# Splitting the weights of 96 projection slabs into high and low parts

## The reference

```python
def first_block(x, ...):
    h = rms_norm(x, norm_gain)
    proj = h @ w_in                                 # 2048 x 8192
    h_conv, b_gate, c_gate, z_conv, q, k, v, z_attn = split(proj)   # 8 parts of 1024
    y_conv = short_gated_conv(h_conv, b_gate, c_gate, conv_w)       # 3 taps
    y_conv = rms_norm(y_conv, conv_out_gain) * silu(z_conv)
    y_attn = attention(rms_norm(q), rms_norm(k), v)                 # 8 heads, causal, 256 keys
    y_attn = rms_norm(y_attn, attn_out_gain) * silu(z_attn)
    return x + concat([y_conv, y_attn]) @ w_out     # 2048 x 2048

def second_block(x, ...):
    h = rmsnorm(x, norm_mix)
    proj = h @ w_in_2                               # 2048 x 7168: conv, state space, gates
    branch_conv = conformer_conv(proj[...])         # 31 taps, layer norm, @ conv_w_out
    branch_ssm = s5_ssm(proj[...])                  # scan, then @ w_val and @ w_gate
    x = x + (gates_a * branch_conv + gates_b * branch_ssm) @ w_out_2
    h = rmsnorm(x, norm_ffn)
    return rmsnorm(x + peer(h), norm_final)         # @ w_q, keys, 128 experts' rows a token from u and v
```

## Time and profile before

| | |
|---|---|
| time, median of 3 runs | 2801.74 us (2801.71 to 2801.96) |
| the profiled execution, its own time | 2801.38 us |
| its span, first to last instruction | 2799.3 us |
| mean granted TensorE clock | 0.869 |
| PE busy | 1950.2 us, 70% |
| DVE busy | 1589.6 us, 57% |
| ACT busy | 279.8 us, 10% |
| POOL busy | 892.0 us, 32% |

### The profile page before, as it was taken

One profiled execution on the slowest core, in us unless ns is written; L12 is line 12 of the kernel. 1 busy time (PEld: TensorE's weight loads), 2 busy tenths in 40 slices (PEclk: granted clock), 3 DMA queues, 4 the chain that ended last, 5 costly groups with the idle time before them and its releaser, 6 DMA issues. The chain is left out here.

```text
span 2799.3 us, 21816 instructions
## 1 busy us (share of the span) xinstructions
PE 1950.2 (70%) x7892; PEld 1459.8 (52%) x7892; DVE 1589.6 (57%) x2475; ACT 279.8 (10%) x593; POOL 892.0 (32%) x525
## 2 busy tenths in 40 slices
PE   8999999999999999999994000077775000057776
PEld 6888888888887888888783000032222000022222
DVE  5012223110886896520157999977547999964444
ACT  1002222101102010200110000000001000000000
POOL 0000000000000000000004888856555888865553
PEclk9999999999998999999997555599998555589999
DMA  7554554554453554455456999999999999999998
GB/s 184 151 149 123 141 143 135 137 149 121 120 151 90 154 146 152 136 163 153 120 134 247 422 422 422 422 421 422 422 422 386 423 422 422 422 421 422 421 421 341
DMA packets 458269, 747.06 MB, mean 267 GB/s; under 512 B 22130, under 2 KB 391236, under 8 KB 392260
## 3 DMA queue, kind: packets, MB, share of 16 engines
q0 software_dynamic: 73728, 536.90, 46.1%
q1 hardware_dynamic: 373248, 207.63, 26.4%
q10 hardware_dynamic: 11204, 1.29, 0.3%
HBM read 743.68 MB, written 2.10 MB: 266 GB/s over the span
## 5 line engine op out<-in xcount | busy, mean ns | idle before, releaser
L366 PE MATMUL ps<-operand,weight_raw 128*128 128x256 f32 x6144 | 1348.9, 382 | 10.0 <-DVE operand L885 9.0
L366 PEld LDWEIGHTS ps<-operand,weight_raw 128*128 128x128 f32 x6144 | 1173.5, 192 | 177.4 <-issue 15.7
L594 PE MATMUL ps<-weight_raw,residual_t 128*128 128x512 f32 x256 | 124.0, 630 | 676.0 <-ACT residual_t L839 637.1
L1316 DVE SCALAR_TENSOR_TENSOR slots<-slots,work 128x2048 f32<-128x2048 f32 x192 | 437.5, 2291 | 29.4 <-DMA slots<-in_peer_u,slots 29.0
L594 PEld LDWEIGHTS ps<-weight_raw,residual_t 128*128 128x128 f32 x256 | 48.5, 199 | 751.4 <-ACT residual_t L839 697.7
L594 PE MATMUL ps<-slots,residual_t 128*128 128x512 f32 x768 | 356.3, 608 | 116.5 <-DMA slots<-in_peer_v,slots 116.0
L326 POOL DMA_INDIRECT slots<-in_peer_u,slots x192 | 395.8, 2062 | 60.5 <-issue 58.9
L319 POOL IOTA slots<- 128x16 f32 x1 | 0.1, 144 | 1232.9 <-DVE operand L1236 1232.9
L1331 DVE SCALAR_TENSOR_TENSOR work<-slots,work 128x2048 f32<-128x2048 f32 x96 | 225.7, 2351 | 220.5 <-DMA slots<-in_peer_v,slots 220.2
L326 POOL DMA_INDIRECT slots<-in_peer_v,slots x192 | 262.4, 1366 | 180.8 <-PE ps L594 143.5
L594 PEld LDWEIGHTS ps<-slots,residual_t 128*128 128x128 f32 x768 | 140.4, 192 | 331.9 <-ACT residual_t L839 170.4
(11 more groups left out here) (197 smaller groups left out, 1078.0 us busy)
## 6 DMA issues: line engine op xcount, KB each, us to landing
weight_raw<-in_w_in SPq DMA_DIRECT2D x120, 1024.0 KB, 6.1
weight_raw<-in_w_out SPq DMA_DIRECT2D x32, 1024.0 KB, 6.0
weight_raw<-in_peer_w_q SPq DMA_DIRECT2D x16, 1024.0 KB, 6.0
weight_raw<-in_ssm_w_val SPq DMA_DIRECT2D x8, 1024.0 KB, 5.2
weight_raw<-in_ssm_w_gate SPq DMA_DIRECT2D x8, 1024.0 KB, 5.2
weight_raw<-in_conv_w_out SPq DMA_DIRECT2D x8, 1024.0 KB, 5.2
slots<-in_peer_u,slots POOLq DMA_INDIRECT x192, 16.5
slots<-in_peer_v,slots POOLq DMA_INDIRECT x192, 15.9
```

The lines of the kernel that those rows point to most:

```text
L366: mm = nc.tensor.matmul(ps_p[:, t % PSLOTS, :], w[:, k, :], operand[:, k, :], start=(k == order[0]), stop=(k == order[-1]))
L594: mm = nc.tensor.matmul(ps_v[:, c, :], diag[:, n, :], rows[n][:, c * 512:(c + 1) * 512], start=False, stop=False, skip_group_check=True)
L1316: v.scalar_tensor_tensor(out=rows[n], in0=rows[n], scalar=1.0, in1=h_tok[:, t, :], op0=ALU.mult, op1=ALU.mult, accum_out=dots[:, at:at + 1 ...
```

## The change

96 of the 192 slabs are computed in another way: the 64 of the first input projection and the 16 of each output projection. A weight w is split into a high part (w stored as float32r, a float32 type of lower precision for products) and a low part (w minus the high part), and so is the operand; the product is then high x high + high x low + low x high. The low x low part is left out.

- ScalarE copies each slab from `weight_raw` to one of two new buffers `weight_high` (`split_high`), always two tiles ahead, and GpSimd writes the low part over the slab itself (`weight_low` lies at the address of `weight_raw`).
- The operand's high part goes to `operand_high`, at the address of `op_b`, by 16 copies on ScalarE; the low part to `operand_low`, in place in `op_a`, by 16 subtractions: on GpSimd for the first stage, on VectorE for the two output projections. For the first output projection the products y stay in their slots instead of going to `op_b`.
- TensorE (`split_product`) issues per tile 32 products of the high weights and then, when the low slab is there, 16 of the low weights.
- The order of the input projection's parts is changed (the gate c before the gate b), the gated convolution of three taps is cut up and its first two parts stand after heads 6 and 7, and TensorE turns the state-space coefficients after tile 14 instead of after tile 23.
- `operand` and the slabs lie next to each other in SBUF, with `weight_high` behind them; the other 96 slabs keep float32.

```diff
+NHIGH = 2
+SPLIT_IN, SPLIT_OUT, SPLIT_OUT2 = 0, 64, 80
+SLAB_OUT2 = 64 + 16 + 56 + 16 + 8
+def split_slab(i):
+    return i if i < SPLIT_OUT2 else SLAB_OUT2 + i - SPLIT_OUT2
-Q0, K0, V0, ZA0, HC0, BG0, CG0, ZC0 = range(0, 64, 8)
+Q0, K0, V0, ZA0, HC0, CG0, BG0, ZC0 = range(0, 64, 8)
+LAM_AFTER = 14
+        with nc.sbuf_tensor("weight_low", [P, NSLAB, SLAB], F32R) as w_low, \
+                nc.sbuf_tensor("operand_low", [P, KD, T], F32R) as o_low, \
+                nc.sbuf_tensor("operand_high", [P, KD, T], F32R) as o_high:
+            pass
         w_raw = sb("weight_raw", [P, NSLAB, SLAB])
+        opnd = sb("operand", [P, 2, KD, T])
+        w_high = sb("weight_high", [P, NHIGH, SLAB], F32R)
...
# GpSimd: ahead of the mask, then behind it
+            for k in range(KD):
+                pool.wait_ge(o_high_ready, k + 1)
+                nc.gpsimd.tensor_tensor(o_low[:, k, :], op_a[:, k, :], o_high[:, k, :], ALU.subtract).then_inc(o_low_ready, 1)
...
+            for i in range(SPLIT_OUT2 + KD):
+                s = split_slab(i)
+                pool.wait_ge(w_high_ready, i + 1)
+                nc.gpsimd.tensor_tensor(w_low[:, s % NSLAB, :], w_raw[:, s % NSLAB, :], w_high[:, i % NHIGH, :],
+                                        ALU.subtract).then_inc(w_low_ready, 1)
...
# TensorE
+            def split_product(i, order=None, ready=None):
+                t = split_tile(i)
...
+                pe.wait_ge(w_high_ready, i + 1)
+                pe.wait_ge(proj_freed, t + 1)
+                for k in order:
+                    if ready is not None:
+                        pe.wait_ge(o_low_ready, ready(k))
+                    nc.tensor.matmul(out, high[:, k, :], o_high[:, k, :], start=(k == order[0]), stop=False)
+                    nc.tensor.matmul(out, high[:, k, :], o_low[:, k, :], start=False, stop=False)
+                pe.wait_ge(w_low_ready, i + 1)
+                for k in order:
+                    mm = nc.tensor.matmul(out, low[:, k, :], o_high[:, k, :], start=False, stop=(k == order[-1]))
+                mm.then_inc(proj_done, 1)
...
             for t in range(24):
-                tile(TILE_IN, t, op_a, ready=(lambda k: (h_scaled, k + 1)) if t == 0 else None)
+                split_product(SPLIT_IN + t, ready=(lambda k: k + 1) if t == 0 else None)
+                if t == LAM_AFTER:
+                    pe.wait_ge(ssm_coef, 1)
...
# ScalarE
+            def split_high(i):
+                s = split_slab(i)
+                act.wait_ge(raw_landed[s % NSLAB], 16 * (s // NSLAB + 1))
+                if i >= NHIGH:
+                    act.wait_ge(proj_done, split_tile(i - NHIGH) + 1)
+                act_copy(w_high[:, i % NHIGH, :], w_raw[:, s % NSLAB, :]).then_inc(w_high_ready, 1)
...
                 square(n, 0, x_t[:, n, :])
+                if n == 11:
+                    split_high(SPLIT_IN)
             root(1, KD, D)
+            split_high(SPLIT_IN + 1)
+            for k in range(KD):
+                act.wait_ge(h_scaled, k + 1)
+                act_copy(o_high[:, k, :], op_a[:, k, :]).then_inc(o_high_ready, 1)
...
             for t in range(24):
                 read_out(TILE_IN, t, slot(t))
+                split_high(SPLIT_IN + t + 2)
...
                 read_out(TILE_IN, t + 1, slot(t + 1))
+                split_high(SPLIT_IN + t + 3)
...
+            act.wait_ge(proj_done, TILE_OUT)
+            for k in range(KD):
...
+                act_copy(o_high[:, dst, :], slot(src)).then_inc(o_high_ready, 1)
...
# VectorE
+            for k in range(KD):
+                src, dst = (Q0 + k, KH + k) if k < KH else (HC0 + k - KH, k - KH)
+                dve.wait_ge(o_high_ready, KD + k + 1)
+                v.tensor_tensor(o_low[:, dst, :], slot(src), o_high[:, dst, :], ALU.subtract).then_inc(o_low_ready, 1)
...
+                if head == HEADS - 2:
+                    dve.wait_ge(proj_freed, freed(BG0))
+                    own.do(v.tensor_tensor(slot(CG0, KH), slot(CG0, KH), slot(HC0, KH), ALU.mult))
+                    conv_tap(2)
+                elif head == HEADS - 1:
+                    conv_tap(1)
```

More of the change, by code:

```diff
@@ L6 @@
 F32 = mybir.dt.float32
+F32R = mybir.dt.float32r
 I32 = mybir.dt.int32
@@ L264, in _ @@
                 load(w_in, 4 * HALF + P * t, TILE_IN + t + 1)
-            for t in range(32, 64):
-                load(w_in, P * t - 4 * HALF, TILE_IN + t + 1)
+            for part in (0, 2, 1, 3):
+                for t in range(KH):
+                    load(w_in, part * HALF + P * t, TILE_IN + len(slab_ends) + 1)
             for t in range(16):
@@ L368, in tile @@
                 mm.then_inc(proj_done, 1)
+            def split_product(i, order=None, ready=None):
+                t = split_tile(i)
+                slabs.append(t)
+                at = split_slab(i) % NSLAB
+                high = w_high[:, i % NHIGH, :].rearrange("p (k n) -> p k n", k=KD)
+                low = w_low[:, at, :].rearrange("p (k n) -> p k n", k=KD)
+                out = ps_p[:, (t - TILE_IN) % PSLOTS, :]
+                order = list(range(KD)) if order is None else order
+                pe.wait_ge(w_high_ready, i + 1)
[9 more added lines that the diff above has]
+                mm.then_inc(proj_done, 1)
             def misc_bank(m, first):
@@ L425, in _ @@
                 for t in range(2):
-                    tile(TILE_IN, 24 + 4 * head + t, op_a)
+                    split_product(SPLIT_IN + 24 + 4 * head + t)
                 pe.wait_ge(v_copied, head + 1)
@@ L437, in _ @@
                                  stop=True).then_inc(scores_done, 1)
-                tile(TILE_IN, 24 + 4 * head + 2, op_a)
+                split_product(SPLIT_IN + 24 + 4 * head + 2)
                 pe.wait_ge(probs_ready, head * 2 + 2)
@@ L443, in _ @@
                 tr.then_inc(probs_turned, 1)
-                tile(TILE_IN, 24 + 4 * head + 3, op_a)
+                split_product(SPLIT_IN + 24 + 4 * head + 3)
                 pe.wait_ge(pt_ready, head + 1)
@@ L452, in _ @@
             for t in range(8):
-                tile(TILE_IN, 56 + t, op_a)
+                split_product(SPLIT_IN + 56 + t)
                 for n in range(4):
@@ L545, in _ @@
             for t in range(16):
-                tile(TILE_OUT2, t, op_a, ready=(lambda k: (merged, k + 1)) if t == 0 else None)
+                split_product(SPLIT_OUT2 + t, ready=(lambda k: 2 * KD + k + 1) if t == 0 else None)
                 if 11 <= t < 15:
@@ L1023, in _, with conv_tap @@
             v.tensor_copy(small[:, 40:41], small[:, 0:1]).then_inc(bdiag_ready, 1)
+            def conv_tap(tap):
+                lag = 2 - tap
+                for n in range(KH):
+                    w = params[:, C_CONV + tap * KH + n:C_CONV + tap * KH + n + 1]
+                    u, y = slot(CG0 + n), slot(HC0 + n)
+                    if lag == 0:
+                        ins = v.tensor_scalar(y, u, w, None, ALU.mult)
+                    else:
+                        ins = v.scalar_tensor_tensor(out=y[:, lag:T], in0=u[:, 0:T - lag], scalar=w, in1=y[:, lag:T],
+                                                     op0=ALU.mult, op1=ALU.add)
+                    own.step(ins)
+                own.wait()
             dve.wait_ge(mask_ready, 2)
@@ L1050, in _ @@
                                     ALU.mult).then_inc(probs_ready, 1)
-            own.n += 4 * HEADS
-            dve.wait_ge(proj_freed, freed(56))
-            own.do(v.tensor_tensor(slot(CG0, KH), slot(CG0, KH), slot(HC0, KH), ALU.mult))
-            for tap in (2, 1, 0):
-                lag = 2 - tap
-                for n in range(KH):
-                    w = params[:, C_CONV + tap * KH + n:C_CONV + tap * KH + n + 1]
-                    u, y = slot(CG0 + n), slot(HC0 + n)
-                    if lag == 0:
-                        ins = v.tensor_scalar(y, u, w, None, ALU.mult)
-                    else:
-                        ins = v.scalar_tensor_tensor(out=y[:, lag:T], in0=u[:, 0:T - lag], scalar=w, in1=y[:, lag:T],
-                                                     op0=ALU.mult, op1=ALU.add)
-                    own.step(ins)
-                own.wait()
+                if head == HEADS - 2:
[4 more added lines that the diff above has]
+                    conv_tap(1)
+            conv_tap(0)
+            dve.wait_ge(proj_freed, freed(ZC0))
             v.tensor_tensor(slot(HC0, KH), slot(HC0, KH), slot(BG0, KH), ALU.mult).then_inc(yconv_raw, 1)
@@ L1236, in _ @@
                 v.tensor_tensor(op_a[:, n, :], slot(GA0 + n), slot(GB0 + n), ALU.add).then_inc(merged, 1)
+                if n >= KH:
+                    operand_low(n - KH)
+            for k in range(KH, KD):
+                operand_low(k)
             add_residual(TILE_OUT2, 56)
```

85 lines of the change are left out of this document (55 added, 30 removed).

## The result

The changed kernel takes 2736.84 us (median of 4 runs, 2736.38 to 2738.26) against 2801.72 (4 runs, 2800.46 to 2801.96): ratio 0.977, 95% interval 0.9753 to 0.9787. It is faster by 65 us, where 134 were forecast. 2736.8 lies in the range, but the forecast itself missed by 69.8 us, and that gap is what the experiments are about. The profiled execution took 2738.26, its span is 2736.5.

A forecast was written before the change was run, and what follows sets the result against it. TensorE bounds the first 1500 us, the DMA 1300 us of expert rows. Terms -151 + 10 + 4 + 3.5 - 1.5 + 2 and -0.4 give -134, so 2801.4 - 134 = 2667 us; range 2640 to 2785.

The forecast's parts named there:

- 93 steady tiles: Changed tiles except three stage starts: 48 products at 110 ns, 5.28 us instead of 6.91, -151 us.
- wait for the coefficients: TensorE's state-space turn at tile 14, reached at 120 us: no wait forecast.
- first tile, read at 46.4: First stage's start: high copy, sixteen operand subtractions, slab subtraction, then low products; +9.8 us (6 to 13).
- output projection's first tile, 11.4: First output projection's start: readout, high slab, sixteen operand pairs, low products; 11.4 us against 7.65, +3.7.
- heads 1 to 7: ScalarE's slab copy before the exponentials fits by 0.6 us; 0.5 us a head put down for seven, +3.5.
- the clock at the starts: Clock lost while TensorE stands at the starts of the first stage and first output projection: +2 us.
- with 256 columns the pass itself covers that load: Changed tile: a float32r product's weight load hides behind its pass, so 110 ns a product was taken.
- Rival C: Changed tiles: a float32r product takes 216 ns, a tile 10.4 us, total 3140 us; chance 0.11.
- Rival A: Changed tiles: each product paced by its own weight load, 126 ns, tile 6.05 us, total 2738 us; chance 0.10.
- now 1.9 later, so no wait: VectorE's coefficients, before at 58.8 us, come 1.9 us later, ahead of TensorE's need at 120.
- rival D: VectorE's 57-instruction coefficient chain and GpSimd exclude each other by whole instructions: 2736 to 2864 us; slow end's chance 0.06.
- 2 us later and they would show: ScalarE's eighteen state-space load issues move to 35 to 46 us, just before the first readout, hidden by 2 us.

The follow-up runs named there:

- e5_bench: Changed kernel plus eight series of back-to-back products of several types and shapes, unread, ahead of the expert part; 2735.13 us in one run.
- e4: Changed kernel with TensorE turning the coefficients after tile 18 instead of 14; 2726.76 us.
- e6: Changed kernel with GpSimd subtracting 8 of 2048 columns and the third product reusing the high weights, low weights left out of the result; 2712.24 us.
- e7: Changed kernel with GpSimd subtracting each slab in four instructions of 512 columns; 2729.04 us.
- e8: Changed kernel with GpSimd making the first low slab before the operand's sixteen low parts; 2723.98 us.
- e10: As e8, with the eighteen state-space loads issued by SyncE after its first four slab loads, rather than by ScalarE; 2731.58 us.
- e9: Changed kernel with ScalarE making the second output slab's high part behind the sixteen operand copies; 2730.57 us.
- e12: Changed kernel with first low slab first, eighteen loads on SyncE, second output slab's high part behind the operand copies, coefficient turn after tile 18; 2716.27 us.

## Why the prediction was right and wrong

The forecast said -134, the medians -64.9. Where the 69 us are, by the prediction's own terms:

| term | forecast | measured | missing |
|---|---|---|---|
| 93 steady tiles, 5.28 us each | -151 | 93 x (5.76 - 6.91) = -107 | 44.6 |
| wait for the coefficients, and the slow products behind it | 0 | 18.56 - 6.30 = 12.3 | 12.3 |
| first tile, read at 46.4 | +9.8 | 51.23 - 36.66 = +14.6 | 4.8 |
| output projection's first tile, 11.4 | +3.7 | 16.0 - 7.65 = +8.3 | 4.6 |
| heads 1 to 7: their 28 tiles above 28 steady ones | +3.5 | (185.65 - 28 x 5.76) - (211.56 - 28 x 6.91) = +6.3 | 2.8 |

The 185.65 and 211.56 us are from ScalarE's readout 28 to its readout 56 (235.12 to 420.77, before 240.54 to 452.10). The rows sum to 69.1. The other terms were small and nearly cancel: head 0, the clock at the starts (+2 forecast; 0.8 in the step behind the first tile, the rest is in the rows above), the second output projection, and the expert part, which took 2.4 us longer in the profiled execution. The 2.4 aren't explained, and are near the noise: the runs of one kernel lie 2 to 9 us apart.

**The new tile failed in size.** The step "with 256 columns the pass itself covers that load" took 110 ns a product from eight transposes; it is 120 to 121 (e5_bench), over the 115 that the prediction itself gave as a sign of being wrong. The rest of the step was right: 48 single-pass products, back to back, nothing waited for. Rival C, 216 ns, is out. Rival A looked to the weight load, and 2738 is nearly the time measured, but that is luck: its sum has 126 ns and no waits, the kernel 120 and 12.3 us lost behind tile 14. The 126 of the earlier trace rows is a pair of load and 128 columns in the plain type; in float32r that pair takes 111. Neither row was of the product's kind: the load records of the transposes take 140 ns, those of the changed products 192. Nor could the plain float32 record have warned, with 217 ns for 213 of pass. What makes the float32r product 13 to 14 ns longer than its pass stays open. The Trainium skill ("TensorE: Matmul & The Clock Gate", section Step-by-step: what each phase is for) says that the next tile's weights load while this tile's matmul runs, and that the load's time follows its column count. In e5_bench the load records agree with the column count (192 ns with 128 float32r columns, 134 with 64), and the overlap is there: without it a product of 256 columns would take the 107 ns of its pass and a load on top. Whether the 14 ns in float32r, against 3 in bf16, are a part of the load that isn't overlapped, no run here shows.

**The coefficients: "now 1.9 later, so no wait" failed.** This was rival D, which had been given 0.06 at its slow end. Its 2736, for a hold of 2.25 us on each of 57 instructions, is the time measured only by luck: it has 69 us of wait where 12.3 were lost, on a sum that was 57 too low elsewhere. The mechanism is real, but the holds fall otherwise: each GpSimd instruction (4.63 us) holds one VectorE instruction to its end, and the others go through in the gap. So the chain gets on by a few instructions for each slab. It starts at 39.8 rather than 32.3 and ends at 142.0 rather than 58.8, 83 us later, of which tile 14's distance covered all but 9.4. e4, e6, e7 and e8 each took the holds or the deadline away in another manner and each lost that wait. The Trainium skill ("SBUF — State Buffer", section Who interferes with whom) says that of VectorE and GpSimd the one that issues first keeps the shared ports for its whole instruction and the other is blocked, and that an instruction of VectorE with two SBUF inputs, or a two-port form of one with a single input, is concerned. Here it holds for both kinds (L1003 and L997, 4.7 us at most), and the additions with one input in PSUM stay at 0.42 throughout. With GpSimd busy for 4.5 of 5.3 us, both in the prediction, that rule would have given, as an estimate, a chain several times as long, and a wait behind tile 14.

**First tile.** Two steps failed. GpSimd's subtraction of 128x256 was put at 0.65 us. GpSimd's timeline:

```profile
28.32 13.54 POOL L337 TENSOR_TENSOR operand_low<-operand,operand_high 128x256 fp32r<-128x256 f32 x16 [25.09 <-ACT operand_high L664]
```

That is 13.54 / 16 = 0.85 us each. They run beside VectorE's scalings, and each holds the other: the scalings went from 6.42 to 12.60 us in all, and GpSimd's last two subtractions, which begin after the last scaling, took 0.72. Sixteen times 0.2 is the first 3. And the sixteen low products came after a wait of 4.7 us, at the lower clock. The stretch from 47.3 to 51.3, where they run:

```profile
47.30:51.30 4.00, 3.89 (x18) 3.89 (x19) 3.97 (x2) 0.07 (x1) 4.00 (x2) 0.50 0.82 93
```

At clock 0.50, which is 1.2 GHz, they start 213 ns apart and take 3.4 us, not 1.8: the rest. "2 us later and they would show", of ScalarE's eighteen issues, was right and the hazard larger than thought: in the changed kernel they end at 50.3, just ahead of the readout; in e6 and e8 they last to 54.5 and do show. With the low slab made first and the issues on another queue (e10) tile 0 is read at 45.8, where the prediction had 46.4.

**Output projection.** The chain was put together as forecast, but VectorE's y products ahead of it were counted at their free price; GpSimd, released by a high copy in their midst, holds them (11.38 against 7.05 us in e9). The sixteen pairs themselves took 5.45 us.

**Right.** ScalarE's and GpSimd's slab work keep up with the tile; DMA at 0.64 to 0.68 of its time and never waited for in the changed tiles; the stages before the expert part pass their gain on: 65.3 us at the last readout before it (1494.3 to 1429.0), 62.8 at the end of the span. With the four edits of e12, the time is 2716.3, 49 from the forecast, of which 44.6 is the one term that no placing can mend, the 120 ns.

## What to carry to other kernels

When a 4-byte product is split into cheaper ones, price each by a measured product of that very type and shape, weight load included: 10 ns too little, 93 x 48 = 4464 times over, was two thirds of this miss. Before work is given to GpSimd, list every chain of VectorE instructions that runs beside it, with two SBUF inputs or of the TENSOR_SCALAR form seen here, and reckon that such a chain moves only in GpSimd's gaps; what counts then is the first deadline at which another engine asks for its end. A wait at such a deadline can cost more than it lasts (12.3 us for 9.4 here), since the products behind it ran at the lower clock. And a kernel that gains by a stall elsewhere (e8) is a hint of a hidden chain, not a result: removing the stall alone made it slower (e10).

## What was not expected of the hardware

- At clock 1.00 a float32r product of 128x128 weights takes 120 to 121 ns with 256 moving columns, 147 with 320, 227 with 512 and 111 with 128; bf16 takes 109 and 56 with 256 and 128. At clock 0.50 the float32r product of 256 columns takes 213 ns, its pass and nothing more.
- VectorE and GpSimd take turns by whole instructions in both directions: sixteen VectorE scalings and sixteen GpSimd subtractions of 128x256 that follow each other took 0.79 and 0.85 us each, where the scalings alone take 0.40 and the subtractions without them 0.72.
- GpSimd's subtraction takes 0.22 us for 128x8, 1.32 for 128x512 and 4.63 for 128x2048, so a cut in four costs about 0.6 us a slab (5.2 for four, back to back).
- One DMA issue on ScalarE's queue took 0.45 us in most places, and the last of eighteen 2.3 or 6.2 us, in which the engine did nothing else.
